# Four changes around the sparse hybrid and the latent attention of a two-block transformer kernel on one core: modulation products in the boundary, order of the weight loads, two background sections a step, and the head norm on VectorE

## The reference, cut to what matters

```python
def adaln_sublayer(x, m, f, ln_g, ln_b):
    shift, scale, gate = m[:, None, 0], m[:, None, 1], m[:, None, 2]
    y = f(x * (1 + scale) + shift)
    return layer_norm(DEEPNORM_ALPHA * x + (1 + gate) * y, ln_g, ln_b)
...
    mod = (cs @ mod_w[layer] + mod_b[layer]).reshape(bsz, N_SUB, 3, D_MODEL)   # cs = silu(c), one row
...
def hybrid_mixer(u, ...):        # 256 x 1024 -> 256 x 1024
    a_q, a_k, a_v, i_q, i_k, i_w, b_qkv, b_a, b_b, b_z = split(u @ w_in)
    out_a = dsa_attention(...)   # 8 heads of 64; an indexer scores the keys, each query takes its best 64
    out_b = gdn_mixer(...)       # short convolution, gated delta rule in chunks of 64, 4 heads of 128
    return concatenate([out_a, out_b]) @ w_out
...
    o = rms_norm(o, norm_g) * silu(z)        # the head norm, at the end of gdn_mixer
...
def mla_mixer(u, ...):           # 16 heads
    c_q, c_kv, k_rope = split(u @ w_in, [384, 640])
    q = rms_norm(c_q, q_norm_g) @ w_q_up
    kv = rms_norm(c_kv, kv_norm_g) @ w_kv_up
    ...                          # rope, chunk-causal attention
    return out @ w_out
```

## Time and profile before

| | |
|---|---|
| time, median of 3 runs | 2393.36 us (2392.84 to 2396.43) |
| the profiled execution | 2387.18 us, its span 2385.3 us, mean granted clock of PE 0.956 |
| PE busy, share of span | 2166.9 us, 91% |
| DVE, ACT, POOL busy | 1374.0 us (58%), 997.9 us (42%), 266.4 us (11%) |
| read from HBM | 407.49 MB, 172 GB/s over the span |
| chain that ended last | PE 73%, DVE 9%, DMA 5%, issue 4%, POOL 4%, ACT 4% |

### The profile page before, as it was taken

One profiled execution on the slowest core, in us unless ns is written; L12 is line 12 of the kernel. 1 busy time (PEld: TensorE's weight loads), 2 busy tenths in 40 slices (PEclk: granted clock), 3 DMA queues, 4 the chain that ended last, 5 costly groups with the idle time before them and its releaser, 6 DMA issues.

```text
span 2385.3 us, 30476 instructions
## 1 busy us (share of the span) xinstructions
PE 2166.9 (91%) x12408; PEld 1775.8 (74%) x12408; DVE 1374.0 (58%) x1986; ACT 997.9 (42%) x1563; POOL 266.4 (11%) x298
## 2 busy tenths in 40 slices
PE   5999888988999999968999978889899988897999
PEld 3777678866778777746767866767799876776997
DVE  3544657846545755645755455656576455665663
ACT  1443353324444444335433434334455344344552
POOL 0000200012000200111210021321000112310000
PEclk9999889988999999989999989999899999998999
DMA  9686473415866876563656653235566552354664
GB/s 307 215 269 230 126 195 107 141 63 185 274 228 202 263 259 207 189 200 124 189 180 200 200 124 105 79 106 166 144 187 193 161 137 71 100 166 115 183 183 138
DMA packets 374491, 412.11 MB, mean 173 GB/s; under 512 B 27511, under 2 KB 319563, under 8 KB 374352
## 3 DMA queue, kind: packets, MB, share of 16 engines
q1 hardware_dynamic: 367216, 388.37, 52.7%
q0 software_dynamic: 7136, 21.81, 2.9%
HBM read 407.49 MB, written 2.62 MB: 172 GB/s over the span
## 4 chain that ended last, share of the span: by engine, by line
PE 73%; DVE 9%; DMA 5%; issue 4%; POOL 4%; ACT 4%; SPq 0%; POOLq 0%; DVEq 0%; ACTq 0%
PE ps L169 70%; PE ps L172 3%; POOL arena L178 3%; DVE arena L178 2%; DVE wlo L178 2%; DMA arena<-in_mod_w 1%; DVE arena L190 1%; ACT whi L175 1%; ACT arena L175 1%; DMA raw<-in_ffn_w_up 1%; POOL small L178 1%; DVE tmp L190 1%; DVE tmp L178 1%; DMA raw<-in_w_up 1%; DMA modrel<-in_mod_b 1%
## 5 line engine op out<-in xcount | busy, mean ns | idle before, releaser
L178 DVE TENSOR_TENSOR wlo<-raw,whi 128x1024 fp32r<-128x1024 f32 (+1 forms) x592 | 720.7, 1237 | 474.2 <-ACT whi L175 471.8
L175 ACT ACTIVATE whi<-raw 128x1024 fp32r<-128x1024 f32 (+1 forms) x592 | 607.2, 1049 | 341.2 <-DMA raw<-in_w_up 87.6
L169 PE MATMUL ps<-whi,uh 128*128 128x512 f32 (+1 forms) x1298 | 539.1, 416 | 56.0 <-ACT arena L175 19.6
L169 PE MATMUL ps<-wlo,uh 128*128 128x512 f32 (+1 forms) x1298 | 516.5, 398 | 0.0
L169 PE MATMUL ps<-whi,ul 128*128 128x512 f32 (+1 forms) x1298 | 417.0, 396 | 0.0
L169 PE MATMUL ps<-whi,arena_r 128*128 128x512 f32 x1184 | 371.9, 392 | 3.5 <-DVE arena_r L178 2.5
L169 PEld LDWEIGHTS ps<-whi,uh 128*128 128x128 f32 x1298 | 251.7, 194 | 145.4 <-issue 41.3
L169 PE MATMUL ps<-uh,whi 128*128 128x256 f32 x984 | 286.0, 291 | 16.9 <-DVE arena L190 13.4
L169 PEld LDWEIGHTS ps<-whi,ul 128*128 128x128 f32 x1298 | 249.0, 193 | 58.2
L169 PEld LDWEIGHTS ps<-wlo,uh 128*128 128x128 f32 x1298 | 252.2, 194 | 51.4 <-issue 0.7
L169 PE MATMUL ps<-ul,whi 128*128 128x256 f32 x984 | 281.7, 286 | 0.0
(11 more groups left out here) (211 smaller groups left out, 1840.9 us busy)
## 6 DMA issues: line engine op xcount, KB each, us to landing
arena<-in_mod_w SPq DMA_DIRECT2D x60, 1024.0 KB, 6.9
raw<-in_w_in SPq DMA_DIRECT2D x90, 512.0 KB, 3.6
raw<-in_ffn_w_gate SPq DMA_DIRECT2D x176, 256.0 KB, 4.0
raw<-in_ffn_w_up SPq DMA_DIRECT2D x176, 256.0 KB, 4.7
raw<-in_ffn_w_down SPq DMA_DIRECT2D x88, 512.0 KB, 4.2
raw<-in_w_up SPq DMA_DIRECT2D x88, 512.0 KB, 3.9
raw<-in_w_down SPq DMA_DIRECT2D x44, 512.0 KB, 3.5
raw<-in_hyb_w_in SPq DMA_DIRECT2D x32, 512.0 KB, 3.9
```

Source lines behind the costliest of these rows:

```text
L169: return Nothing() if self.raw is None else self.raw.matmul(out, l, r, start=start, stop=stop)
L175: return Nothing() if self.raw is None else self.raw.activation(out, src, func, **kw)
L178: return Nothing() if self.raw is None else self.raw.tensor_tensor(out, a, b, op)
```

## The change

1. The boundary always has the two modulation products. Their groups for the hybrid and mla use the two `arena` rooms of the ffn stages and are loaded at the end of the stage before. HYB_FRONT becomes 7, z uses banks 6 and 7, and the two sums stand behind z. In mla two of the four front products are gone, one modulation product each stands behind `mlaq` c = 0 and 1, and `mlaq` and `kv` rotate over four banks.
2. SP asks for the unit of `sm` and three units of conv1 before the modulation load that waits for `x_pool`. In mla SP has two loads fewer in its front.
3. SPLIT_FIRST says how many of four units are split before the second half of the boundary: 4 for an ffn, none for the hybrid, 2 for mla.
4. `tick` runs `rate` steps, 2 in q, k and v of the hybrid and else 1, on each engine.
5. POOL multiplies the gate by the gain ahead of the sums, and DVE does the two multiplications per t that are left.

```diff
@@ -155,11 +155,11 @@
     def tick(self):
-        self.beat = not self.beat
-        if len(self.back) > 1 or self.back and (self.beat or not self.slow):
-            g = self.back.pop(0)
-            if next(g, self) is not self:
-                self.back.append(g)
+        for _ in range(self.rate if self.back else 0):
+            if self.back:
+                g = self.back.pop(0)
+                if next(g, self) is not self:
+                    self.back.append(g)
...
 def stage_groups(n):
@@ -775,9 +775,11 @@
     n = (gi - 8) // 12
     rooms = mod_rooms(M, n)
     i = gi - stage_groups(n)[0]
-    if n >= 0 and KIND[n] == "mla" and i < MLA_FRONT:
+    if i < 2 and n > 0:
+        rooms = mod_rooms(M, 0)
+    elif n >= 0 and KIND[n] == "mla" and i < MLA_FRONT:
         rooms = [M.area(8192 + r * 2048, KD, 256) for r in range(2)]
-    if n >= 0 and KIND[n] == "hybrid" and i < HYB_FRONT:
...
@@ -1281,17 +1283,17 @@
     return e.on("x_pool", n, t) if n < 5 else e.on("x_dve", n, t)
-def mods_between(n):
-    return n + 1 < 6 and KIND[n + 1] == "ffn"
+SPLIT_FIRST = dict(ffn=4, hybrid=0, mla=2)
 def pe_out(pe, M, n):
-    if mods_between(n):
-        pe_mod(pe, M, 7)
+    pe_mod(pe, M, 7)
     pe_into(pe, M, n, 0)
-    if mods_between(n):
-        pe_mod(pe, M, 6)
+    pe_mod(pe, M, 6)
...
-    if mods_between(n):
-        act_mod(act, M, 6)
-    act_unit(act, M, LATE)
+    act_mod(act, M, 6)
+    act_unit(act, M, SPLIT_FIRST[KIND[n + 1]])
     act_stats(act, M, n)
     act_turn_in(act, M, n, 1, U_BANKS[1])
+    act_unit(act, M, LATE - SPLIT_FIRST[KIND[n + 1]])
     for t in range(T):
         act_norm(act, M, n, t)
...
-    if mods_between(n):
-        dve_mod(dve, M)
-        dve_mod(dve, M)
-    dve_unit(dve, M)
+    dve_mod(dve, M)
+    dve_mod(dve, M)
+    first = SPLIT_FIRST[KIND[n + 1]]
+    dve_unit(dve, M, min(first, 1))
     dve_residual(dve, M, n, 1)
-    dve_unit(dve, M, LATE - 1)
+    dve_unit(dve, M, first - min(first, 1))
     dve_into(dve, M, n, 1, m)
     for t in range(T):
         dve_bias(dve, M, n, t)
     dve_turn_in(dve, M, n, 1, U_BANKS[1])
+    dve_unit(dve, M, LATE - first)
```

```diff
-def dve_head_norm(dve, M, tag, o, room):
...
         q = norm_squares(room, t)
...
-    for t in range(T):
-        yield
-def pool_head_norm(pool, M, tag, o, gain, gate, need):
-    for t in range(T):
+    dve.wait_ge(*dve.on("hn_p", tag))
+    for t in range(T):
+        dve.tt(o[:, t], o[:, t], M.hn[:, 4 * t:4 * t + 4].unsqueeze(2).broadcast_to([P, 4, P]), ALU.mult).then_inc(
+            *dve.step("hn_v"))
+        dve.wait_ge(*dve.prev("hn_v"))
+        dve.tt(o[:, t], o[:, t], gate[:, t, :].rearrange("p (h d) -> p h d", h=4), ALU.mult).then_inc(
+            *dve.ev("hn_o", tag, t))
+        yield
+def pool_head_norm(pool, M, tag, gain, gate, need):
+    pool.each(*need)
+    for t in range(T):
+        g = gate[:, t, :].rearrange("p (h d) -> p h d", h=4)
+        pool.tt(g, g, gain.unsqueeze(1).broadcast_to([P, 4, P]), ALU.mult)
         yield
     pool.wait_ge(*pool.on("hn_v", tag, 1))
     pool.ts(M.hn, M.hn, 1.0 / 128, 1e-6, ALU.mult, ALU.add).then_inc(*pool.step("hn_p"))
     pool.wait_ge(*pool.prev("hn_p"))
-    pool.tt(M.hn, M.hn, M.neghalf.broadcast_to([P, 8]), ALU.pow).then_inc(*pool.step("hn_p"))
-    pool.each(*need)
-    for t in range(T):
-        pool.wait_ge(*pool.prev("hn_p"))
-        pool.tt(o[:, t], o[:, t], M.hn[:, 4 * t:4 * t + 4].unsqueeze(2).broadcast_to([P, 4, P]), ALU.mult).then_inc(
-            *pool.step("hn_p"))
-        pool.wait_ge(*pool.prev("hn_p"))
-        pool.tt(o[:, t], o[:, t], gain.unsqueeze(1).broadcast_to([P, 4, P]), ALU.mult).then_inc(*pool.step("hn_p"))
-        pool.wait_ge(*pool.prev("hn_p"))
-        pool.tt(o[:, t], o[:, t], gate[:, t, :].rearrange("p (h d) -> p h d", h=4), ALU.mult).then_inc(
-            *pool.ev("hn_p", tag, t))
-        yield
+    pool.tt(M.hn, M.hn, M.neghalf.broadcast_to([P, 8]), ALU.pow).then_inc(*pool.ev("hn_p", tag))
+    yield from blank(2)
...
+Z_BANKS, MOD_SUMS = (6, 7), (3, 2)
 def pe_hybrid(pe, M, second_half):
     H = Hybrid(M)
     w, uT, ready = H.w, M.uT, u_ready(pe, 0)
     pe.wait_ge(*pe.on("ld_rows"))
-    tr(pe, M, fill(pe, M, 6, ("cw",))[:, 0:48], H.rows).then_inc(*pe.ev("cw_tr"))
-    pe_tok_halves(pe, M, [("z", w, 3664, 4176, (4, 5), lambda t: [("z_gate", t)])], 0, second_half)
+    tr(pe, M, fill(pe, M, 5, ("cw",))[:, 0:48], H.rows).then_inc(*pe.ev("cw_tr"))
+    pe_tok_halves(pe, M, [("z", w, 3664, 4176, Z_BANKS, lambda t: [("z_gate", t)])], 0, second_half)
+    for b in MOD_SUMS:
+        pe_mod_sum(pe, M, b)
     pe_feat(pe, M, "conv0", w[:, :, 2120:2632], 512, uT, ready, lambda i: ("conv", i))
...
@@ -1727,15 +1734,17 @@
     pe.back.append(pe_indexer(pe, M, H))
     while "delta_set" not in pe.flags:
         pe.tick()
+    pe.rate = 2
     pe_feat(pe, M, "q", w[:, :, 0:512], 512, uT, ready, lambda i: (by_turns(i), "q", i))
     pe_feat(pe, M, "k", w[:, :, 512:1024], 512, uT, ready, lambda i: (by_turns(i), "k", i))
     pe_tok(pe, M, "v", w, 1024, 1536, uT, KD, ready, lambda t: ("pj_act", "v", t))
+    pe.rate = 1
     pe.back.append(pe_chosen(pe, M, H))
     for _ in hybrid_rest(pe):
...
@@ -2453,22 +2469,18 @@
     pe_tok_halves(pe, M, [("c0", L.w, 0, 512, (4, 5), lambda t: [("pj_act", "c0", t)]),
                           ("c1", L.w, 512, 672, (6, 7), lambda t: [("pj_act", "c1", t)])], 3, second_half)
     mark(pe, M, 4, "up")
-    pe_mod(pe, M, 3)
-    pe_mod(pe, M, 2)
+    pe.banks = four
     pe_mod_sum(pe, M, 1)
     pe_mod_sum(pe, M, 0)
     pe_mod(pe, M, 3)
     pe_mod(pe, M, 2)
     pe_flip(pe, M, "ct", L.cb, 5, (0, 1, 2), [pe.on("mla_v", "norm", 1)], lambda j: [("flip_dve", "ct", j)])
-    pe_mod(pe, M, 3)
     ct = [pe.on("flip_dve", "ct", 2)]
     for c in range(3):
-        if c:
-            pe_mod_sum(pe, M, 1)
-            pe_mod_sum(pe, M, 0)
-        if c == 1:
+        pe_tok(pe, M, ("mlaq", c), L.wq, c * 512, c * 512 + 512, L.cT, 3, ct, lambda t: ("pj_act", "mq", c, t))
+        if c < 2:
+            pe_mod_sum(pe, M, c)
             pe_mod(pe, M, 3)
-        pe_tok(pe, M, ("mlaq", c), L.wq, c * 512, c * 512 + 512, L.cT, 3, ct, lambda t: ("pj_act", "mq", c, t))
     for c in range(4):
         pe_tok(pe, M, ("kv", c), L.wkv, c * 512, c * 512 + 512, L.cT[:, 3:5, :], 2, ct, lambda t: ("pj_act", "mv", c, t))
     by = lambda tag: lambda j: [("flip_dve", tag, j) if j % 2 else ("flip_act", tag, j)]
@@ -2479,7 +2491,9 @@
         if i in MLA_MODS:
             pe_mod_sum(pe, M, 7)
             pe_mod(pe, M, 6)
+    pe.banks = (4, 5)
```

```diff
-    for b in (3, 2, 3, 2):
-        act_mod(act, M, b)
+    act.banks = (4, 5, 6, 7)
+    act_mod(act, M, 3)
+    act_mod(act, M, 2)
     act_unit(act, M, 6)
     for j in range(3):
         act_flip_hi(act, M, "ct", j, 5, L.cT, (0, 1, 2))
-    act_mod(act, M, 3)
     for c in range(3):
-        if c == 1:
+        if c:
             act_mod(act, M, 3)
         act_tok(act, M, ("mlaq", c), 3, 512, keep(("mq", c), lambda t: L.Q[:, t, c * 512:c * 512 + 512], scale=96 ** -0.5))
...
-    for _ in range(4):
-        dve_mod(dve, M)
+    dve.banks = (4, 5, 6, 7)
     dve_mod_fix(dve, M, 1)
     dve_mod_fix(dve, M, 0)
+    dve_mod(dve, M)
+    dve_mod(dve, M)
...
@@ -3638,7 +3653,9 @@
             sp_ffn(sp, M, n)
             ready = []
         elif KIND[n] == "hybrid":
-            sp_mods_open(sp, M, n, sp.on("x_pool", 0, T - 1))
+            sp_units(sp, M, 4)
+            sp_mod(sp, M, sp.todo.pop(0), sp.on("x_pool", 0, T - 1))
+            sp_mods_next(sp, M)
             for place in "abc":
                 sp_upto(sp, M, n, place)
                 sp_mods_next(sp, M)
@@ -3646,16 +3663,17 @@
             sp.wait_ge(*sp.on("used", M.uid["v"]))
             ready = [sp.on("flip_dve", "B", 1)]
...
         else:
-            sp_mods_open(sp, M, n, sp.on("used", M.uid[("s", 3), "y"]))
+            sp_mod(sp, M, sp.todo.pop(0), sp.on("used", M.uid[("s", 3), "y"]))
+            sp_mods_next(sp, M)
             sp_upto(sp, M, n, "up")
-            for _ in range(MLA_FRONT - 2):
+            for _ in range(MLA_FRONT - 4):
                 sp_mods_next(sp, M)
             sp_upto(sp, M, n, "out")
...
-        if n < 5 and KIND[n + 1] == "ffn":
+        if n < 5:
             sp_mods_open(sp, M, n + 1, *ready)
         sp_upto(sp, M, n + 1, "in")
```

More of the change, by code:

```diff
@@ L124, in __init__ @@
         self.met, self.steps = {}, 0
-        self.back, self.beat, self.slow = [], False, False
+        self.back, self.rate = [], 1
         self.unit, self.lag, self.flags = 0, 0, set()
@@ L1090, in sp_ffn @@
     C = course(n)
-    if n and mods_between(n - 1):
+    if n:
         sp_mods_next(sp, M)
@@ L1585, in norm_squares, with dve_head_norm @@
     return room[t].rearrange("p a s -> p (a s)").rearrange("p (h d) -> p h d", h=4)
-def dve_head_norm(dve, M, tag, o, room):
+def dve_head_norm(dve, M, tag, o, room, gate):
     for t in range(T):
@@ L1737, in pe_hybrid @@
```

(11 more changed lines are left out.)

35 lines of the change are left out of this document (20 added, 15 removed).

## The result

The kernel became slower: 2405.62 us (median of 12 runs, 2399.42 to 2412.99) against 2393.1 us (12 runs), a ratio of 1.0055 with an interval of 1.004 to 1.0071. My forecast was 2371, in a range of 2355 to 2386.

The account below looks back on a forecast made before the run. PE, busy 91% of its span, was taken as the bound; 11.6 (front) + 2.5 (hybrid from q on) + 8 (mla) = 22.1 us less than 2393.36 gave 2371.3, stated as 2371, range 2355 to 2386.

Parts of the forecast that it names:

- I share them: 86 us there, and 38 us for the attention: Hybrid from q on: 124 us of PE work at full clock, 86 in q, k, v, 38 in attention with products and transposes.
- the wait of 7.7 us: Before the first attention step: PE waits 7.7 us for DVE's head norm (5.5 us) and splits.
- that of 4.0 for the loads: Hybrid's end: a new 4.0 us wait, as the last modulation product's load needs the room of the product before.
- the fourth: Rival, 0.14: slower; DVE bounds q, k, v, and the uncovered attention waits each step at half clock, 19 to 38 more.
- My bound of 8 more: Hybrid from q on, slow bound: 8 us more if the attention, standing alone, waits at every step at half clock.
- The third rival: Whole kernel: every named wait goes and none comes, about 35 to 40 us less, 2356; chance 0.13.
- The front: Boundary 0 to 1 and hybrid's front: shorter waits and a higher clock, 11.6 us less, bounds 7 and 15.
- The 3.1 us that I gave to the clock behind z: Hybrid's front, 283.4 to 321.6 us: a little under half of up to 6.8 us gain from a higher clock.
- mla: Boundary 3 to 4 and mla: `mlaq` starts 0.6 us earlier, banks give 7.4; 8 us less, bounds 3 and 14.
- The bank term of 7.4 us: mla behind `mlaq`'s start: four banks instead of two end PE's 8.1 us of waits for ACT, keeping 0.7.
- mla keeps its wait: Rival, 0.17: `kv_norm_g`'s load holds DVE and transposes, DVE becomes releaser; mla gives 0, total 14 less, 2379.
- The norm: Hybrid's end: PE's 8.36 us wait for the head norm on POOL is gone with POOL's six multiplications.

Follow-up runs that it names:

- filler: The changed kernel with four matmuls of 128x128 of constants added on PE after each step of the attention: 2398.22 us, ratio 1.0028.
- two steps alone: The kernel before with only `tick` and the `rate` lines changed, two steps a tick in q, k and v: 2427.81 us, ratio 1.0159.
- mla as before: The changed kernel with the boundary 3 to 4 and mla of the kernel before: 2410.5 us, ratio 1.007.
- two steps in q and k alone: The changed kernel with two steps a tick in q and k and one in v: 2379.24 us, ratio 0.9935.
- one step: The changed kernel with `rate` 1 in q, k and v on each engine: 2369.54 us, a second time 2376.73; median of all 12 runs 2374.3.

## Why the prediction was wrong, step by step

**The step that failed** is "I share them: 86 us there, and 38 us for the attention", the hybrid from q on, summed as 2.5 us less. In the trace it is 27.2 more. The sum took 124 us of PE's work at full clock and never asked whether the clock would stay. It had the evidence: the end before, with the attention over and the delta rule alone, already stood at 0.63. The attention from its first step to the output product took 62 us instead of 50.8 with its waits; at a mean of 0.59, 82% of 63 us ran at half, 26 us lost. q, k and v took 116 us instead of 96: 11 us of waits (I had 10) and a clock of 0.73 over v's 43.5 us, 54% of them at half, 12 us lost. The two clock terms make 38 us, the waits in q, k and v were sized about right, the wait of 7.7 us was 4.5, and that of 4.0 for the loads did not come: 32 us, against the 30 (27.2 and 2.5) that the term was off. The attention's term is in all four traces with two steps in v and no filler (0.59 to 0.60 from its first row to the output product). That of v is not: in two of them (two steps alone, and mla as before) v stands at 0.95. The split of the 124 us was off by some 5 (91 us of work at full clock in q, k and v, not 86), and the sum counts the last 1.1 us of transposes twice, as the 38 us hold them already.

**The rival that came true** is the fourth, which I gave 0.14, and only in part: the attention falls to half clock when too little stands between its steps. It does not wait for ACT and DVE at each step, as the rival has it; its rows follow one another. And DVE as the bound in q, k and v costs 2 to 5 us (two steps in q and k alone). My bound of 8 more named the same fall to half clock that the rival prices at 19 to 38, so the bound was too small by my own working; with the row of 0.63 the fall should have been the base case. (The third rival's terms add up to 43 us and not to the 35 to 40 it gives; nothing hangs on it.)

**The front** was right in size and mostly in mechanism: 9.1 us less by the start of q against 11.6. ACT's 12.41 us of the earlier trace rows are gone, the wait inside conv0 is 1.65 (I had 2.9) and that for product a is 2.31 (I had 1.9). The first wait of the boundary is 2.27 instead of 1.1, the second gone instead of 1.9. The 3.1 us that I gave to the clock behind z did not come: behind the wait in conv0 the changed kernel is 11.9 us ahead, and at the modulation product behind `sm`, after the wait for product a, 7.9.

**mla** was 8 us less, and is nothing to 3. Its first step was right: the waits for `in_mod_w` go and one of 15.09 comes for `kv_norm_g`, as forecast. The bank term of 7.4 us failed: I read PE's waits for ACT as waits for a bank, and did not look at what ACT waited for in the same stretch of the kernel before (1037 to 1076 us), which was DVE:

```profile
ACT arena L175 <- DVE arena L193: 14.4, 5, 4.4
```

Of the 7.4 us, 3 are left with four banks against two. The rival "mla keeps its wait" named DVE as the releaser and gave 0; for this part it was the right one, by another chain than its reason.

In the changed kernel the transposes `ct` stand between a wait and `mlaq`, and the first 4 us of `mlaq` ran at half clock, as its first row shows (0.76 us, against 0.48 for the same matmul before, which had a modulation product between):

```profile
1055.61 0.76 PE L169 MATMUL ps<-whi,uh 128*128 128x512 f32 x1 [1.36 <-issue]
```

By the rule that I had cited from the Trainium skill (TensorE: Matmul & The Clock Gate, Part 4: PE-mode transpose: a transpose does not count as busy in the same way) 1.7 us were to come back. The trace agrees in size: by the aligned instructions the changed kernel is 18.6 us behind at the first matmul of `mlaq` and 20.5 behind 4 us later, 1.9 lost. It does not show that the transposes are the reason, as PE stood idle for 15.09 us ahead of them.

**The norm** was to give 8.36 us at the hybrid's end. With two steps it gives nothing, since POOL's work hides behind the attention as well, and with one step 3.9. **The mixers** are unchanged within the scatter: from mla's output to the last product it is 1239.7 us before and 1240.3 after.

## What to carry to other kernels

When a change packs background work closer, price what it leaves uncovered as well as what it fills: short dependent matmuls that ran at full clock beside larger ones can run at half clock alone, and PE's busy share does not show it. Look at the order too: here the same matmuls ran at half clock or at full clock, depending on where the independent products stood among them. Where one engine waits for a second, look up what the second waits for before giving it more buffers. And look for single loads behind a long wait in one queue: one line of SP's order was worth some 10 us here, two small loads of POOL's 7.

## What the runs showed that I had not expected

Added work made the kernel faster: 7.4 us less for 48 useless matmuls, by which the granted clock rose from 0.59 to 0.93.

The same kernel scatters by its clock. One step's two traces are 13.6 us apart, with identical instructions: 5.2 us at the hybrid's output, some 3 behind the first mixer, and some 9 more in the second mixer. The second mixer, in each:

```profile
1960.00:2070.00 110.00, 94.15 (x494) 74.77 (x493) 66.86 (x113) 41.41 (x79) 37.82 (x37) 0.95 0.30 86
```

```profile
1966.00:2082.00 116.00, 99.88 (x471) 78.99 (x469) 64.87 (x108) 39.27 (x74) 37.74 (x37) 0.85 0.27 79
```

A granted clock of 0.95 in one and 0.85 in the other. Medians of 6 runs of one kernel came out 7 us apart (2369.54 and 2376.73), so effects under 5 us were read here from the place in the trace and not from the time. A place scatters too, by 3 us from q to the hybrid's output in the two traces of one step, by 9 in v with two steps and by 3 in mla, so that the 3.9 us of the norm and the 3 of the banks are sizes from one pair of traces each. Why the clock of equal instructions differs from run to run stays open, and so does the 2.70 us wait at the boundary 2 to 3 of the changed kernel (1.14 before), whose instructions the change does not touch.
